# A decoder block on eight cores: weight blocks in the heads, first loads, squares, residual loads and activation tracking are reordered

## The reference, cut to what matters

```
h    = rmsnorm(x) * g1                       # x (8, 2048, 2048) float32
proj = h @ w_in                              # attn q|k|v (12 heads of 128), mlstm q|k|v|o (4 heads), 8 gate columns
attn = dilated_attention(rope(rmsnorm(q)), rope(rmsnorm(k)), v)   # windows 128, 512, 2048 with dilations 1, 4, 16
qk   = silu(causal_dwconv(mlstm q|k))        # 4 taps
hm   = rmsnorm(mlstm(qk, mv, gates) * sigmoid(mo))                # chunks of 128 positions
x    = x + concat(attn, hm) @ w_out
h2   = rmsnorm(x) * g2
u    = causal_dwconv(h2 @ w_up)              # 3 taps, 2 * 5632 columns
x    = x + (silu(gate) * val) @ w_down       # gate, val = halves of u
```

## Time and profile before

| | before |
|---|---|
| runs | 3881.02, 3551.95, 3419.8 us (median 3551.95) |
| profiled execution | 3421.72 us; the span of its slowest core is 3420.7 us |
| spans of the eight cores | 3401.2 to 3420.7 us |
| mean granted TensorE clock | 0.965 to 0.971 of full speed |
| TensorE busy | 3161.2 us (92% of the span) |
| VectorE, ScalarE, GpSimd busy | 1542.9, 1036.3, 168.4 us |
| moved by DMA | 313.16 MB, mean 92 GB/s |

### The profile page before, as it was taken

How to read it: one execution, slowest core, us unless ns; L and a number is a source line. 1 busy time by engine, 2 the same in 40 slices (tenths; PEclk the granted TensorE clock), 3 DMA queues, 4 the chain that set the end, 5 groups by cost and what they waited for, 6 DMA issues and landing times.

```text
span 3420.7 us, 45125 instructions; the slowest of 8 cores (3401.2 to 3420.7 us)
## 1 busy us (share of the span) xinstructions
PE 3161.2 (92%) x16712; PEld 1554.8 (45%) x16712; DVE 1542.9 (45%) x2084; ACT 1036.3 (30%) x1678; POOL 168.4 (5%) x200
## 2 busy tenths in 40 slices
PE   5999998877877886999999999999999999999999
PEld 3544553444444453444444444444444444444444
DVE  4234564555554652113766666400056666662000
ACT  3223664544554553333222222100012222220000
POOL 0000001111111110000000000000000000000000
PEclk9999999988998998999999999999999999999999
DMA  9222223122113118675333444566553333335564
GB/s 257 41 47 38 47 51 89 41 47 63 39 43 68 39 41 201 166 181 161 74 74 75 79 81 81 121 135 138 117 111 74 74 74 74 74 75 104 120 141 103
DMA packets 133976, 313.16 MB, mean 92 GB/s; under 512 B 65664, under 2 KB 85120, under 8 KB 119680
## 3 DMA queue, kind: packets, MB, share of 16 engines
q0 software_dynamic: 14400, 174.69, 27.6%
q1 hardware_dynamic: 119360, 135.58, 13.6%
HBM read 433.02 MB, written 51.90 MB: 142 GB/s over the span
## 4 chain that ended last, share of the span: by engine, by line
PE 87%; DMA 5%; ACT 3%; DVE 2%; issue 2%; SPq 1%; DVEq 0%; ACTq 0%; POOLq 0%; POOL 0%
PE ps L988 36%; PE ps L1030 18%; PE ps L680 10%; PE ps L921 5%; PE ps L331 4%; DMA wslot<-w_qk 3%; PE ps L411 3%; PE ps L320 2%; PE ps L438 1%; PE ps L756 1%; PE ps L766 1%; SPq L179 1%; PE ps L769 1%; DMA arena<-xA 1%; DMA arena<-xT 1%
## 5 line engine op out<-in xcount | busy, mean ns | idle before, releaser
L988 PE MATMUL ps<-arena,wslot 128*128 128x512 bf16 x5632 | 1215.9, 379 | 0.0
L988 PEld LDWEIGHTS ps<-arena,wslot 128*128 128x128 bf16 x5632 | 551.0, 98 | 664.4
L1002 DVE SCALAR_TENSOR_TENSOR arena<-arena,cfs 128x1024 f32<-128x1024 f32 x352 | 452.1, 1284 | 295.0 <-ACT arena L999 210.4
L680 PE MATMUL ps<-big,wslot 128*128 128x512 bf16 x1536 | 383.5, 395 | 139.0 <-DMA wslot<-w_qk 139.0
L1030 PE MATMUL ps<-big,wslot 128*128 128x512 bf16 x2048 | 456.6, 381 | 13.1 <-DVE arena L1006 13.1
L999 ACT ACTIVATE arena<-arena,cfs 128x1024 f32<-128x1024 f32 x176 | 217.0, 1233 | 456.8 <-DVE arena L991 450.4
L1030 PEld LDWEIGHTS ps<-big,wslot 128*128 128x128 bf16 x2048 | 201.2, 98 | 258.3 <-issue 19.6
L1041 DVE TENSOR_TENSOR arena<-ps,arena 128x512 f32<-128x512 f32 x64 | 44.3, 692 | 570.3 <-PE ps L1030 570.3
L991 DVE TENSOR_TENSOR arena<-ps,arena 128x512 f32<-128x512 f32 x352 | 242.9, 690 | 127.1 <-PE ps L988 107.9
L680 PEld LDWEIGHTS ps<-big,wslot 128*128 128x128 bf16 x1536 | 151.8, 102 | 300.9 <-issue 162.0
L921 PE MATMUL ps<-big,wslot 128*128 128x512 bf16 x960 | 222.2, 385 | 10.8 <-DMA big<-mixd 10.8
(11 more groups left out here) (126 smaller groups left out, 2652.8 us busy)
## 6 DMA issues: line engine op xcount, KB each, us to landing
wslot<-w_up POOLq DMA_DIRECT2D x44, 2048.0 KB, 12.6
wslot<-w_down POOLq DMA_DIRECT2D x32, 1408.0 KB, 10.7
arena<-vd SPq DMA_DIRECT2D x36, 512.0 KB, 11.5
arena<-xA SPq DMA_DIRECT2D x8, 2048.0 KB, 19.1
arena<-xT SPq DMA_DIRECT2D x64, 256.0 KB, 4.7
x1d<-arena SPq DMA_DIRECT2D x64, 256.0 KB, 3.5
arena<-x1d SPq DMA_DIRECT2D x64, 256.0 KB, 6.4
outT<-arena SPq DMA_DIRECT2D x64, 256.0 KB, 4.4
```

The lines of the kernel that those rows point to most:

```text
L680: K.mm([lambda e, kc=kc: e.matmul(bank[:], sl[:, kc, part * 128:(part + 1) * 128], hT[:, kc, tt * TT:(tt + 1) * TT], start=(kc == 0), stop ...
L988: K.mm([lambda e, kc=kc: e.matmul(ps[bi][:], sl[:, kc, c0:c0 + 128], h2p[:, kc, t2 * TT:(t2 + 1) * TT], start=(kc == 0), stop=(kc == KC - ...
L1002: K.op(dve, lambda e, k=k: e.scalar_tensor_tensor(out=a, in0=y[:, k:k + HS], scalar=wc(k), in1=a, op0=ALU.mult, op1=ALU.add), [B_yy, B_cf, ...
```

## The change

Six edits:

- Heads: the filler generator is run to its end (49 instead of 48), so block 8 is issued ahead of head 0. The last head issues no block, and the output projection issues one more at its step 6. From head 0 on, each `w_issue` at a head's end is for the block after the next.
- First loads: x tile 0 (in four quarters), the first half of `w_mvg`, x 1, the second half, x 2, x 3, `w_v[0]` and `cb` all go through GpSimd's queue in this order, without waits between them; only `cf` goes through SP. `w_mvg` is laid out as two halves with a buffer each. x 4 to 7 go through SP as before.
- Squares: those of tile tt+2 are issued in four pieces between the four half groups of tile tt, and so one tile ahead of `norm_tile(tt+2)`. Half groups rotate over four PSUM banks. The first tiles run in another order: tile 0, its first halves, tile 1, its first halves, then the second halves of both, then tile 2. Value groups start from tile 3. `hT` is tracked by quarters of the features (four buffers to each tile).
- Residual loads: the first four `xr` loads are issued ahead of the four `mix` loads on SP, where they were behind them.
- Activation: one buffer to each of the 44 chunks. A down group waits for the 22 chunks that it reads.

```
-    blocks = [(KC * 520, w_mvg), (KC * 512, w_v[0]), ...
+    blocks = [None, (KC * 512, w_v[0]), ...
...
-    xload(0)
-    w_issue()
     K.dma(sp, cf[:], cfd, B_cf, True)
-    xload(1)
-    sp.wait(B_ws[0].w)
-    xload(2)
-    xload(3)
-    pool.wait(B_xs[3].w)
+    B_mvh = [K.buf("mvh%d" % i) for i in range(2)]
+
+    def mvload(hh):
+        K.dma(pool, wslots[0][:, hh * KC * 260:(hh + 1) * KC * 260], w_mvg[hh], B_mvh[hh], True)
+
+    xload(0, pool)
+    mvload(0)
+    xload(1, pool)
+    mvload(1)
+    wstate["issued"] = 1
+    xload(2, pool)
+    xload(3, pool)
     w_issue()
     K.dma(pool, cb[:], cbd, B_cb, True)
+    B_ws[0].w = B_mvh[1].w
...
+    def square(tt, q):
+        K.op(act, lambda e: e.activation(out=sqA[tt % 2][:, 4 * q:4 * q + 4, :], in_=xs[tt % 4][:, 4 * q:4 * q + 4, :],
+                                         func=AF.Square), [B_x[tt][q]], [B_sqA[tt % 2][q]])
...
-    norm_tile(0)
-    for tt in range(NTA):
+    for tt in range(2):
+        for q in range(4):
+            square(tt, q)
+        norm_tile(tt)
+        mv_group(2 * tt, 0)
+        mv_group(2 * tt + 1, 0)
+    for q in range(4):
+        square(2, q)
+    for tb in range(4):
+        mv_group(tb, 1)
+    norm_tile(2)
+    for q in range(4):
+        square(3, q)
+    for tt in range(2, NTA):
         if tt + 1 < NTA:
             norm_tile(tt + 1)
-        mv_group(2 * tt)
-        mv_group(2 * tt + 1)
-        if tt >= 4:
+        for n in range(4):
+            mv_group(2 * tt + n // 2, n % 2)
+            if tt + 2 < NTA:
+                square(tt + 2, n)
+        if tt >= 3:
             v0_next(2)
+    inherit(B_ws[0], B_mvh)
     w_issue()
...
-        while fstate["done"] < 48 and fstate["done"] + 1 <= fstate["due"] + 1e-6:
-            next(fil)
+        while fstate["done"] < 49 and fstate["done"] + 1 <= fstate["due"] + 1e-6:
+            next(fil, None)
...
-            w_issue()
+            if h < NHA - 1:
+                w_issue()
         else:
...
+            xr, B_xr = zip(*[A.new("xr%d" % i, 65536 + i * 2048, TT, F32) for i in range(4)])
+            for i in range(4):
+                K.dma(sp, xr[i], xT[i * 128:(i + 1) * 128, 0:TT], B_xr[i], True)
             for b in list(att["B_ost"]) + [B_hmst]:
                 sp.wait((b.dsem, b.dcnt))
...
-        if i % 16 == 15:
+        if i % 16 == 15 or i == 6:
             w_issue()
...
-    B_actT = G.buf("actT", 0, 65536)
+    B_act = [G.buf("act%d" % c, c * 2048, 2048) if c < 32 else None for c in range(NFC)]
...
-                     [B_ag, B_av], [B_actT])
+                     [B_ag, B_av], [B_act[cp]])
...
-                          for k in range(22)], [B_slot, B_actT], [B_ps[bi]])
+                          for k in range(22)], [B_slot] + B_act[kh * 22:kh * 22 + 22], [B_ps[bi]])
```

More of the change, by code:

```diff
@@ L247, in bc_ap @@
         return bass.AP(base.tensor, base.offset, [list(base.ap[0])] + [list(d) for d in dims])
-    blocks = [(KC * 520, w_mvg), (KC * 512, w_v[0]), (KC * 512, w_mqk[0]), (KC * 512, w_mqk[1]), (KC * 512, w_mo),
+    blocks = [None, (KC * 512, w_v[0]), (KC * 512, w_mqk[0]), (KC * 512, w_mqk[1]), (KC * 512, w_mo),
               (KC * 512, w_v[1]), (KC * 512, w_v[2])]
@@ L310, in build @@
+    xload(3, pool)
     w_issue()
     K.dma(pool, cb[:], cbd, B_cb, True)
+    B_ws[0].w = B_mvh[1].w
     slot_m, B_slot_m = w_next()
-    slm = slot_m[:].rearrange("p (k n) -> p k n", n=520)
+    slm = [slot_m[:, hh * KC * 260:(hh + 1) * KC * 260].rearrange("p (k n) -> p k n", n=260) for hh in range(2)]
     slot_v, B_slot_v = w_next()
[L317 to L327, removed]
@@ new lines, in mv_group @@
+    def mv_group(tb, hh):
+        bi = 2 + rot["mv"] % 4
+        rot["mv"] += 1
+        for q in range(4):
+            K.mm([lambda e, kc=kc: e.matmul(ps[bi][:, 0:260], hT[:, kc, tb * 128:(tb + 1) * 128],
+                                            slm[hh][:, kc, :], start=(kc == 0), stop=(kc == KC - 1))
+                  for kc in range(4 * q, 4 * q + 4)], [B_mvh[hh], B_hTq[tb // 2][q]], [B_ps[bi]])
+        K.op(act, lambda e: e.activation(out=mvt[:, tb, hh * 256:(hh + 1) * 256], in_=ps[bi][:, 0:256],
+                                         func=AF.Copy), [B_ps[bi]], [B_mv])
+        K.op(dve, lambda e: e.tensor_tensor(out=gt[:, tb, hh * 4:hh * 4 + 4], in0=ps[bi][:, 256:260],
+                                            in1=cf[:, CF_BG + hh * 4:CF_BG + hh * 4 + 4], op=ALU.add),
+             [B_ps[bi], B_cf], [B_gt])
@@ L345, in norm_tile @@
         for q in range(4):
-            K.op(act, lambda e, q=q: e.activation(out=sq_t[:, 4 * q:4 * q + 4, :], in_=x_t[:, 4 * q:4 * q + 4, :],
-                                                  func=AF.Square), [B_x], [B_sq[q]])
-        for q in range(4):
             K.mm([lambda e, kc=kc: e.matmul(ps[pb][:, 0:TA], ones, sq_t[:, kc, :], start=(kc == 0), stop=(kc == KC - 1))
-                  for kc in range(4 * q, 4 * q + 4)], [B_sq[q], B_ones], [B_ps[pb]])
+                  for kc in range(4 * q, 4 * q + 4)], [B_sqA[tt % 2][q], B_ones], [B_ps[pb]])
         K.op(act, lambda e: e.activation(out=rs_t, in_=ps[pb][:, 0:TA], func=AF.Ln, scale=1.0 / D, bias=EPS),
@@ L681, in proj_half @@
                                         hT[:, kc, tt * TT:(tt + 1) * TT], start=(kc == 0), stop=(kc == KC - 1))
-              for kc in range(8 * half, 8 * half + 8)], [B_slot, B_hTt[2 * tt], B_hTt[2 * tt + 1]], [B_bank])
+              for kc in range(8 * half, 8 * half + 8)], [B_slot] + B_hTq[2 * tt] + B_hTq[2 * tt + 1], [B_bank])
         if half == 0:
@@ L890, in build @@
     NST = 6
-    xr, B_xr = zip(*[A.new("xr%d" % i, YO + i * 2048, TT, F32) for i in range(NST)])
+    xr2_, B_xr2_ = zip(*[A.new("xr%d" % i, YO + i * 2048, TT, F32) for i in range(4, NST)])
+    xr, B_xr = xr + xr2_, B_xr + B_xr2_
     x1t, B_x1t = zip(*[A.new("x1t%d" % i, YO + 12288 + i * 2048, TT, F32) for i in range(NST)])
@@ L973, in build @@
                 yi += 1
-                if hf == 0 and cp == 32:
-                    inherit(B_actT, old_h)
+                if B_act[cp] is None:
+                    B_act[cp] = A.buf("act%d" % cp, 32768 + (cp - 32) * 2048, 2048)
                 for gv in range(2):
```

57 lines of the change are left out of this document (31 added, 26 removed).

## The result

The changed kernel takes 0.9416 of the time of the kernel before, 95% interval 0.9389 to 0.9443: faster, by 5.8%. Its profiled execution takes 3219.13 us against 3421.72, 203 us less; 3191 was forecast. Its spans are 3199.6 to 3218.1 us, the slowest on core 2, and its mean granted clock 0.992 to 0.995 instead of 0.965 to 0.971. The medians of all runs (3221.31 and 3485.88) hold runs in which some cores had a lower mean clock, as cores 4 to 7 had in the profile of hold_w_out, so only runs and cores without it are compared.

What follows compares the result with a forecast made beforehand. TensorE, busy 92% of the span, was taken as the bound, so only its waits and low clock could be won: 164 + 25 + 24 + 18 = 231 us off 3421.72 gives 3191, 6.7% less, range 3160 to 3305.

Steps and rivals of the forecast that it cites:

- the rival of colliding DMAs: First loads or mix loads collide in the DMA engines: 27 us less gain, 3218 us; chance 0.08.
- Heads: Head projections: 139.0 us of w_qk waits and 25 us of slow clock go, 164 us; bounds 80 and 170.
- First stage: Norm and value stage: earlier first loads and squares end it at 159 or 162, not 187.33; 25 us, bounds 12 and 38.
- Start of the output projection: After attention: waits for mixd and a residual tile go with slow restarts; 24 us, bounds 10 and 27.
- Down projections: Both down projections: 13.1 us of waits for the last activation and 4.7 of slow restarts go; 18 us, bounds 13 and 18.
- the heads' chain: Rival in the heads: attention's chain through ScalarE and VectorE still bounds them, half of 164 kept, 3273 us; chance 0.12.
- the falling clock: Slower rival: clock falls inside the heads; half a head at low clock costs 300 us, 3490 us; chance 0.02.
- the signs named for being wrong: New ScalarE or VectorE waits in heads; squares waiting for x 2 or x 3 beyond 50; L938 waiting on a residual tile.
- those for being right: No w_qk wait, 50 us heads, clock near 1.00; value stage by 162; output step within 3 us; down projections 304, no wait.
- The estimate from the Trainium skill: First loads: at 2.0 us and 436 GB/s x 0 and half of w_mvg land by about 12; sum some 5 us lower.

Runs made afterwards that it cites:

- hold_w_out: Changed kernel with the second w_out block held until the last mix load landed; cores 0 to 3: gap under 0.1 us, output projection 237.1 to 241.7 us.
- heads_only: Kernel before with the heads' block count alone changed; ratio 0.9525 (0.9497 to 0.9552).
- late_block8: Changed kernel with block 8 issued in head 0 behind its eighth half group; profiled execution 3219.53 us, median head stage 590.3 against 592.0.
- x4_pool: Changed kernel with x 4 to 7 on GpSimd's queue behind the first loads, instead of SP; first stage's median end 172.1 us, 3.8 later.
- x45_first: Changed kernel with x 4 and x 5 on GpSimd's queue ahead of w_v and cb; first stage ends at 165.6 us in the median, 2.7 earlier.
- xr_only: Kernel before with only the four residual loads moved ahead of the mix loads; ratio 0.9973 (0.9962 to 0.9985).
- act_only: Kernel before with one buffer for each activation chunk alone; ratio 0.9968 (0.9957 to 0.998).
- late_h2: Changed kernel with the 4 MB h2 reload moved behind the first down projection's second column block; 3217.32 us, first down projection 303.9 to 304.1.
- sp_first: Changed kernel with x 0 to 3 on SP instead of GpSimd's queue; first stage ends at 191.1 us, 22.8 later.

## Why the prediction was right, and where it was off

The direction and the range held, and each term had its sign; 28 us of 231 were not there, and the third term came out above the second. The measured 3219 is 1 us from the figure of the rival of colliding DMAs (3218). That is luck in the number: the rival took 13 us from the first stage and 14 from the output projection, and the runs show 7, 2, and the rest in head 0 and the down projections, which it left alone. Its mechanism is what was missing all the same.

- Heads, 164 forecast, 155.9 measured on the slowest core. Both parts of the term were right: no wait for `w_qk`, clock at 1.00, no new wait of any length on ScalarE or VectorE behind head 0, heads of 50.5 us where 50 were said. The eleven heads behind head 0 gain 161.5, or 14.7 for each seam where 14.9 were counted. Head 0 loses 5.6. The step said what the moved load no longer hides from, and not what it now flies beside; for blocks 9 to 18 that is nothing critical, for block 8 it is a table and a store with a single buffer (heads_only, late_block8). The 139.0 us were core 3's; the other cores had waited 123.2 to 133.6, and the median core gains 152.5.
- First stage, 25 forecast, 17.8 measured. The period of 15.8 us was met to a tenth. The mis-sized term is the start, up to tile 2. Some of it is x 3, at 58.1 where 45 to 52 were counted: with x 4 coming in on another queue x 3 is waited for, and without it not (x4_pool), but x 4 needs its place ahead of `w_v` (x45_first). That is worth 2.7 us or somewhat more by x45_first, where 4.9 of the 25 are still missing (185.7 - 165.6 is 20.1). The rest lies ahead of x 3: the first value matmuls at 21.6 and not 18, x 1's squares behind their evictions, VectorE's tile 1 from 34.2 and not 30, and the second halves done at 51.9 and not 46, at a granted clock of 0.79 for which the sum had no term.
- Start of the output projection, 24 forecast, 22.0 measured. Mix tile 0 came 1.8 us late, within the 1311 to 1313 of the forecast. Residual tile 4, for which 2 us to spare were counted, was late by some 3.5 us, and three short waits of L971 (5.4 us) follow. That the step needs both parts was counted right: heads_only leaves the residual's wait, xr_only the mix tile's.
- Down projections, 18 forecast, 7.6 measured. This step failed. It said "Next is the eviction, no wait in the rows", and looked for what is late next in VectorE only. Next was the weight block whose flight the old stall had covered (act_only, late_h2). It cost 7.5 us in the first half's down projection, more than the 6.0 that the up stage ahead of it had won; against the 303.9 without the wait (late_h2) it is 9.2, most of what the term lacks.
- Of the rivals, the heads' chain and the falling clock didn't come: the granted clock in the heads is 1.00. What the Trainium skill (TensorE: Matmul & The Clock Gate, A second HAM failure mode: psum-queue depth-cycling) describes, a clock that falls by short idle times between groups on cycling PSUM banks, doesn't come up here: two banks alternate, the idle time is 13 us in 515, and the clock holds. The collision of DMAs did come, in three places: x 3 (2.7 us in the median), head 0 (5.6 on the slowest core) and `w_down` (9.2 on the slowest core).
- Of the signs named for being wrong, two showed, both small: squares waited for x 3 beyond 50 us (58.1), and the norm's matmul of the output projection (L938, now L971) waited on a residual tile. Of those for being right, the value stage ended at 169.4 on the slowest core and not by 162, and one down projection had a wait ahead.
- The estimate from the Trainium skill (DMA: Bandwidth & Descriptors, Anatomy of one DMA), x 0 and half of `w_mvg` by about 12 us, didn't hold, with all eight cores loading: squares of x 0's last quarter start at 14.6 and the first value matmuls at 21.6.

## What to carry to other kernels

Follow an issue in its own engine's queue, not in program order of the kernel: the load was late because its issue stood behind copies, and one block more in hand made the same place early by a head. When a stall is removed, list every transfer that was in flight under it, with its issue, its landing and its new reader: the stall at the down projection had hidden `w_down`. When a load is moved, ask both what it now flies beside and whether it is still in time: block 8 has been too early for a store and too late for head 1. And when loads are moved ahead, put them into one queue in the order of their use, up to the first that is not urgent: what shares the engines from another queue can take more than its half, as in sp_first.

## What the runs showed of the hardware that was not expected

Sharing between two queues was far from equal in bytes. In sp_first x 0's quarters (0.5 MB, 4 KB for each partition) are on SP while weight loads with rows of 16 KB and more are on GpSimd's queue; a quarter then takes about 11 us (17.64, 28.25, 39.50), some 48 GB/s, while the core as a whole moves 199 GB/s from 10 to 39 us, as counted at the destination. In one queue the same quarters follow each other in about 1.3 us (squares at 13.31 and 14.61). In the kernel before, x 0 as a single load with 16 KB for each partition had landed at 18.7 beside the same weights.

The DMA view of sp_first from 10 to 39 us, core 5, shows what was equal (queue: packets, MB, share of the engines; q0 is GpSimd's, q1 SP's):

```profile
q0 software_dynamic: 421, 3.97, 80.9%
q1 hardware_dynamic: 426, 1.81, 20.2%
```

The two queues moved the same number of packets within about 1%, of 9.4 and 4.2 KB in the mean, and on the other seven cores from 10 to 36 us it is the same (346 to 365 packets on each queue). The Trainium skill (DMA: Bandwidth & Descriptors, Queues, rings and completion order) says that an engine takes turns between queues by packet; these counts agree with it. So the queue with the small packets gets the small share. No run changed the size of x 0's pieces alone, so that larger pieces would have cured sp_first is not shown.
